# Where the first three pieces of the last modulation are made: in the retention's third head, or beside the collecting of the first layer's expert results

## The chip, the cores and the metric

The kernel runs on one core of one Trainium2 chip, in one launch. The metric is the device time of that launch in microseconds. A core has TensorE (PE in the profile), with its weight loads shown apart as PEld, VectorE (DVE), ScalarE (ACT), GpSimd (POOL) and SyncE (SP), which here only issues DMAs. Sixteen DMA engines move data between the chip's memory and the on-chip buffers.

## The reference, cut to what matters

Two blocks follow each other on 512 tokens of width 1024. The first has forgetting attention with a hierarchical mixture of experts (layer 0), then retention with a second mixture (layer 1). The second block has two layers with adaptive modulation, and a context of 256 tokens beside them.

```python
# first block, each layer i
h = h + mixer_i(rms_norm(h, norm_mix[i]))        # forgetting attention, then retention
h = h + hier_moe(rms_norm(h, norm_ffn[i]), ...)  # 32 experts, each token goes to two of them

# second block
sc, sc_ctx = jax.nn.silu(c), jax.nn.silu(c_ctx)
for layer in range(DEPTH):
    mod = sc @ ada_w[layer] + ada_b[layer]       # 1024 x 3072 weights: shift, scale, gate
    shift, scale, gate = jnp.split(mod[:, None, :], 3, axis=-1)
    mod_c = sc_ctx @ ada_w[layer] + ada_b[layer]
    ...
    u = rms_norm_2(h, norm_g[layer]) * (1 + scale) + shift
```

The modulation depends on `c_2`, `c_ctx_2` and `ada_w_2` alone. It can be made at any time before the second block reads it. `ada_w_2[1]`, the modulation of the last layer, is 12 MB in float32, and the kernel makes it in six pieces of 512 columns (2 MB each), numbered 0 to 5.

## The kernel before, in words

**Stages.** The program is a list of stages (`timeline`). `run` (L3242) goes through them on each of PE, ACT, DVE and POOL: at the start of a stage an engine waits until the other engines are done with the stage before (less a slack that some stages have), then it does its part, drains and counts itself done. SP has no such waits: it works through the `sp` parts in order, and what it issues waits by itself for the semaphores that free the destination.

**The weight ring.** Mixer weights pass through a ring of three slots of 2 MB. `Weights.add` gives a unit its number in the order of use. `Weights.load` (L232) waits until the unit three before it has been read, and then issues the DMA (L236). All loads come from SP, so they are issued in that order, behind one another. The experts' stage uses the same three slots beside five in `arena`; for the units behind it `freed` says that a slot is free once the last expert weight in it has been read. For the first of the three slots that is the down projection of expert 30, for the others the two halves of the up projection of expert 31.

**Products.** A `Products` stage holds jobs: PE fills a PSUM bank (`fill`), and DVE or ACT takes it (`take`). PE works through the jobs in their order and so does each taker.

**One piece of modulation** (`modulation`, L2578) is two jobs, both taken by DVE. `rows`: 32 matmuls of 32 columns of weights (`cmod`) against 128 of the piece (L2590; the profile has 64, two for each in float32), then a copy of the 128x128 result into `XT` (L2593), in one of two buffers. The second, whose place in the order the caller chooses: PE turns the copy (L599), and DVE adds the bias into `modc` (L2598). Filling frees the ring slot.

**Order around the change.** Layer 0 ends with `Experts` (32 experts, 64 rows each, weights streamed from memory). PE's last work there is the down projections of experts 30 and 31 (L2184); ACT copies each result (L2282), POOL scatters it to `y_dram` (L2156), and ACT's part of the stage ends when the scatters of experts 30 and 31 have landed. ACT also stores the context's gate projection (`context_z`, 1 MB) at the end. Then comes `CombineNorm` (`cb0`): SP waits for the experts' stage to be done (L2361) and fetches the results in four pieces of 1 MB, one for each tile of 128 tokens (L2364). DVE adds both expert rows to `H` (L2390, two instructions for each tile), ACT squares, DVE makes the root, both scale the rows, PE turns them (L2413) and ACT and DVE write them to `XT`. Then the retention begins.

**The retention** goes head by head: the stage `ret{h}` projects values and gate (twelve or more groups of 16 matmuls, L689), the stage `rn{h}` makes the retention itself (from L2704 on) with the next head's queries and keys in between, and `ro{h}` projects out (L818). In the third head (h = 2) pieces 0, 1 and 2 of the modulation stand among the projections. In the last head's `rn3` pieces 3, 4 and 5 stand in the retention, in the order rows, rows, turn, rows, turn, turn.

Of the kernel before, what the change touches and what calls it, by code (L numbers as in the profile page):

```python
# [23 lines left out]
KC = D // P  # L24
# [7 lines left out]
RET_H, RET_DK, RET_DV = 4, 256, 512  # L32
# [90 lines left out]
def build(nc, io):  # L123
    ctx = ExitStack()
    with ctx:
# [117 lines left out]
        class Stage:  # L243
# [25 lines left out]
            def pe(self, pe): pass  # L269
# [3 lines left out]
            def sp(self, sp): pass  # L273
# [2092 lines left out]

        class CombineNorm(Combine):


            ROWS, JUNK = region(2 * NT * D, NT, D), region(3 * NT * D, D)  # L2370

# [14 lines left out]
            def dve(self, dve):  # L2386
                for t in range(NT):
                    dve.wait_ge(self.s(f"got{t}"), self.at(f"got{t}") + 16)
                    for k in range(2):
                        i = dve.scalar_tensor_tensor(H[:, t, :], self.YG[:, t, k, :], gates[:, k, t:t + 1], H[:, t, :], ALU.mult, ALU.add)  # L2390
                        if k == 0:
                            dve_step.then(dve, i)
                    i.then_inc(self.s("summed"), 1)
                for g in range(2):
                    w = slice(2 * g, 2 * g + 2)
                    ms, t_, y, r = (st[:, j, w] for j in range(4))
                    dve.wait_ge(self.s("squares"), 2 * g + 2)
                    dve_step.then(dve, dve.tensor_scalar(ms, ms, 1.0 / D, EPS, ALU.mult, ALU.add))
                    root_of(dve, ms, y, t_, r)
                    dve.nop().then_inc(self.s("rstd"), 1)  # L2400
                    t = 2 * g + 1
                    dve.tensor_scalar(self.ROWS[:, t, :], H[:, t, :], st[:, 3, t:t + 1], None, ALU.mult).then_inc(self.s("rows_v"), 1)
                for c in range(1, KC, 2):
                    dve.wait_ge(self.s("turned"), c + 1)
                    dve.tensor_scalar(XT[:, c, 0:SEQ], bank(c), cols[:, V_MIX + KC + c:V_MIX + KC + c + 1], None, ALU.mult)

            def pe(self, pe):
                for t0 in range(0, NT, 2):
                    pe.wait_ge(self.s("rows_a"), t0 // 2 + 1)
                    pe.wait_ge(self.s("rows_v"), t0 // 2 + 1)  # L2410
                    for c in range(KC):
                        for t in range(t0, t0 + 2):
                            i = pe.transpose(bank(c)[:, t * P:(t + 1) * P], self.ROWS[:, t, c * P:(c + 1) * P], ident)  # L2413
                        if t0 + 2 == NT:
                            i.then_inc(self.s("turned"), 1)
# [128 lines left out]
        def use_units(stage, *us):  # L2544

            def sp(eng):
                for u in us:
                    Weights.load(eng, u)
            stage.sp = sp
# [123 lines left out]
        def moe(layer, after):  # L2673
            route = next(stage for stage in timeline if stage.tag == ("fo1", "ro3")[layer])
            lane = ContextValues("late", 1) if layer else ContextMixing("early", 0)
            Experts(f"ex{layer}", layer, after, route, lane.inline())
            (CombineNorms if layer else CombineNorm)(f"cb{layer}", lane)


        R_ROT, R_DEC = region(20480, 2, SEQ), region(21504, RET_H, SEQ)  # L2680
# [87 lines left out]
        def retention():  # L2768
            w = io["ret_w_in"][0]

            def modulation_unit(q):
                return Weights.add((0, KC, 512, io["ada_w_2"][1][:, 512 * q:512 * (q + 1)]))

            def qk_unit(h):
                return Weights.add((0, KC, 256, w[:, 256 * h:256 * (h + 1)]), (2048, KC, 256, w[:, D + 256 * h:D + 256 * (h + 1)]))

            def queries_keys(p, qk, tables=None, then=None, lead=False):
                sevens.split += (qk,)

                def turn_pairs(dve, s, m, sums, plus):  # L2780

                    if tables and (s, m) == (0, 0):
                        dve.wait_ge(*tables)
                    if plus is not None:
                        dve_step.then(dve, dve.tensor_tensor(R_SUM, sums, plus, ALU.add))
                        sums = R_SUM
                    cos, sin = (R_ROT[:, a, 256 * s:256 * (s + 1)].unsqueeze(1).broadcast_to([P, 2, 256]) for a in range(2))
                    dve.tensor_tensor(R_COS, sums, cos, ALU.mult)
                    dve_step.then(dve, dve.tensor_tensor(R_SIN, sums, sin, ALU.mult))
                    dst = (R_Q, R_K)[m][:, :, 256 * s:256 * (s + 1)]  # L2790
                    dve.tensor_tensor(dst[:, 0, :], R_COS[:, 0, :], R_SIN[:, 1, :], ALU.subtract)
                    return dve.tensor_tensor(dst[:, 1, :], R_SIN[:, 0, :], R_COS[:, 1, :], ALU.add)
                sevens.unit(qk, False, hook=turn_pairs, then=then, lead=lead)

            quad = lambda at: region(at, 4, 256)
            sevens = Sevens((quad(13312), quad(14336), quad(19456), quad(2048)), quad(24576), quad(25600))
            for h in range(RET_H):
                p = Products(f"ret{h}")
                last = h == RET_H - 1
                modulated = h == RET_H - 2  # L2800
                qk = [] if h else [qk_unit(0)]
                m0 = modulation_unit(0) if modulated else None
                uv = Weights.add((0, KC, 512, w[:, 2 * D + 512 * h:2 * D + 512 * (h + 1)]))
                m1 = modulation_unit(1) if modulated else None
                ug = Weights.add((0, KC, 512, w[:, 4 * D + 512 * h:4 * D + 512 * (h + 1)]))
                m2 = modulation_unit(2) if modulated else None
                use_units(p, *(u for u in (*qk, m0, uv, m1, ug, m2) if u is not None))
                if h == 0:
                    loads(p, (R_ROT, io["rot"]), (R_DEC, io["decay"]))
                    sevens.split += (qk[0],)  # L2810
                    sevens.begin(p).weight_sums(qk[0], tokens=True)
                    queries_keys(p, qk[0], (p.s("small"), p.at("small") + 32), lambda: sevens.weight_sums(uv), True)
                else:
                    sevens.begin(p).weight_sums(uv)
                if last:
                    p.pool = lambda pool: route_weights(pool, 1)
                if modulated:
                    turned = modulation(p, m0, 1, 0)
                sevens.unit(uv, True, whole(R_V), then=lambda: sevens.weight_sums(ug), lead=(h > 0))
                if modulated:  # L2820
                    turned()
                    turned = modulation(p, m1, 1, 1)
                sevens.unit(ug, True, whole(R_G), func=ACT.Silu)
                if modulated:
                    turned()
                    modulation(p, m2, 1, 2)()

                inner = Products(f"rq{h}", width=4).inline()
                if not last:
                    qk = qk_unit(h + 1)  # L2830
                    use_units(inner, qk)
                    sevens.split += (qk,)
                    sevens.begin(inner).weight_sums(qk)
                    lead = len(inner.jobs)
                    queries_keys(inner, qk)
                    first = sevens.middle
                else:
                    lead = 0
                    ms = [modulation_unit(3 + i) for i in range(3)]
                    use_units(inner, *ms)  # L2840
                    turned = None
                    for i, m in enumerate(ms):
                        then = modulation(inner, m, 1, 3 + i)
                        if turned:
                            turned()
                        turned = then
                    turned()
                    first = len(inner.jobs)
                r = Retain(f"rn{h}", h, inner, lead, first)
                u = Weights.add((0, 4, D, io["ret_w_out"][0][512 * h:512 * (h + 1), :]))  # L2850
                where = dict(bank0=4, ready=r.laid())
                o = RouteProj("ro3", 1, u, 4, R_YT, **where) if last else OutProj(f"ro{h}", u, 4, R_YT, NT, **where)
                o.slack = {("pe", "dve"): 1}
                use_units(o, u)
# [436 lines left out]
```

## Time and profile before

| | |
|---|---|
| median of 3 runs | 2964.3 us (2963.15 to 2972.04) |
| the profiled execution | 2958.9 us |
| its span | 2957.1 us |
| PE, PEld, DVE, ACT, POOL busy | 91%, 59%, 39%, 22%, 10% |
| mean granted TensorE clock | 0.966 |
| moved by DMA | 610 MB, mean 206 GB/s |

The times of all rows are microseconds from the start of the span. A releaser behind an arrow is what ended the idle time before an instruction. A share of the chain of waits says how much of the span hangs on an engine: PE has 74% of it, DMA 11% and DVE 6%.

### The profile page before, as it was taken

What the parts mean: (1) busy time and instruction counts of PE and PEld (TensorE: products, weight loads), DVE (VectorE), ACT (ScalarE), POOL (GpSimd) and SP (SyncE); (2) the same over time, 40 slices, a digit from 0 to 9 for tenths busy, and PEclk for the clock granted to TensorE, in tenths of its full rate; (3) what the DMA queues carried; (4) which work ended last, traced back from release to release, by engine and by line L of the source; (5) the groups of instructions that cost most, each with busy time, mean ns of one, the idle gap of its engine ahead of it and who ended that gap; (6) DMA issues with size and microseconds to landing.
All of it is one profiled execution on the core that took longest, in us unless ns stands there. A gap on an engine that the chain in (4) does not pass through costs nothing.

```text
span 2957.1 us, 35044 instructions
## 1 busy us (share of the span) xinstructions
PE 2686.4 (91%) x14222; PEld 1738.8 (59%) x14222; DVE 1140.6 (39%) x2541; ACT 640.4 (22%) x1316; POOL 289.8 (10%) x280
## 2 busy tenths in 40 slices
PE   7999979999999699999979989997699998999998
PEld 5858743554444476776743444443577667865864
DVE  4344441112122544424341111110755455665566
ACT  2130421123222100100020010000353341043053
POOL 2002000111110000001000111110200001212211
PEclk9999989999999899999989999999899999999999
DMA  5603248999998521232378999997310111320310
GB/s 182 263 10 136 115 183 353 417 414 414 378 417 364 212 86 63 80 126 101 133 289 363 421 420 420 416 419 329 124 45 31 66 38 57 97 82 14 112 26 36
DMA packets 115354, 610.19 MB, mean 206 GB/s; under 512 B 13148, under 2 KB 25500, under 8 KB 88432
## 3 DMA queue, kind: packets, MB, share of 16 engines
q1 hardware_dynamic: 92000, 541.98, 46.0%
q0 software_dynamic: 20512, 54.76, 5.5%
q10 hardware_dynamic: 2672, 11.09, 1.0%
q8 instruction: 117, 1.92, 0.3%
q14 instruction: 53, 0.43, 0.0%
HBM read 588.84 MB, written 35.65 MB: 211 GB/s over the span
## 4 chain that ended last, share of the span: by engine, by line
PE 74%; DMA 11%; DVE 6%; PEld 3%; issue 2%; ACT 2%; POOLq 0%; PEldq 0%; SPq 0%; DVEq 0%; ACTq 0%; POOL 0%
PE psum L689 24%; PE psum L2172 12%; PE psum L2184 6%; DMA ring<-in_expert_w_gu 6%; PE psum L818 6%; PE psum L944 5%; PE psum L589 4%; DMA arena<-in_expert_w_gu 4%; PE psum L973 3%; PE psum L962 3%; PE psum L579 2%; PE psum L1239 2%; PEld psum L689 2%; PE psum L2165 1%; PE psum L2178 1%
## 5 line engine op out<-in xcount | busy, mean ns | idle before, releaser
L2172 PE MATMUL psum<-ring,XT 128*64 128x512 f32 x1024 | 242.1, 612 | 24.1 <-DMA ring<-in_expert_w_gu 21.1
L2172 PE MATMUL psum<-arena,XT 128*64 128x512 f32 x1024 | 237.9, 608 | 15.7 <-DMA arena<-in_expert_w_gu 15.6
L2243 DVE TENSOR_TENSOR XT<-XT,psum 64x512 f32<-64x512 f32 x64 | 44.1, 690 | 529.5 <-ACT XT L2246 529.5
L689 PE MATMUL psum<-arena 128*128 128x256 f32 x1056 | 238.7, 379 | 0.0
L689 PEld LDWEIGHTS psum<-arena 128*128 128x128 f32 x1056 | 200.3, 190 | 27.1
L944 PE MATMUL psum<-arena 64*128 64x384 f32 (+7 forms) x736 | 187.4, 473 | 27.1 <-ACT arena L998 16.2
L689 PE MATMUL psum<-XT,ring 128*128 128x256 f32 x864 | 195.3, 380 | 5.3 <-DVEq L3250 5.3
L689 PEld LDWEIGHTS psum<-XT,ring 128*128 128x128 f32 x864 | 163.3, 190 | 32.2 <-issue 6.8
L2172 PEld LDWEIGHTS psum<-ring,XT 128*64 128x64 f32 x1024 | 74.8, 140 | 168.5 <-issue 129.6
L818 PE MATMUL psum<-ring,arena 128*128 128x512 f32 x384 | 166.6, 593 | 4.4 <-DVEq L3250 2.0
L2172 PEld LDWEIGHTS psum<-arena,XT 128*64 128x64 f32 x1024 | 76.7, 139 | 154.5 <-issue 131.7
L998 ACT ACTIVATE arena<-psum,rt 128x768 f32<-128x768 f32 (+4 forms) x192 | 144.0, 750 | 44.0 <-DVE rt L3157 26.1
L986 ACT ACTIVATE arena<-psum 128x512 f32<-128x512 f32 (+3 forms) x304 | 133.1, 477 | 92.7 <-PE psum L962 91.2
L2156 POOL DMA_INDIRECT y_dram<-XT,lists x64 | 64.5, 1008 | 868.1 <-ACT XT L2282 840.7
L2246 ACT ACTIVATE XT<-psum 64x512 f32<-64x512 f32 x64 | 37.8, 590 | 506.9 <-PE psum L2172 506.9
L962 PE MATMUL psum<-cst,arena 128*128 128x128 f32 x880 | 135.6, 282 | 10.8 <-DVE arena L1042 5.8
L709 ACT ACTIVATE XT<-psum 128x512 f32<-128x512 f32 x33 | 19.7, 597 | 579.4 <-PE psum L689 579.4
L689 PE MATMUL psum<-ring,XT 128*128 128x256 f32 x624 | 141.0, 380 | 3.9 <-DVEq L3250 2.9
L962 PEld LDWEIGHTS psum<-cst,arena 128*128 128x128 f32 x880 | 99.5, 143 | 57.0 <-issue 31.6
L689 PEld LDWEIGHTS psum<-ring,XT 128*128 128x128 f32 x624 | 118.0, 190 | 22.3 <-PEq L3250 3.6
L689 PE MATMUL psum<-ring,arena 128*128 128x256 f32 x576 | 129.5, 379 | 1.0 <-DVEq L3250 1.0
L689 PE MATMUL psum<-arena,ring 128*128 128x256 f32 x576 | 130.2, 379 | 0.0
(382 smaller groups left out, 3779.2 us busy)
## 6 DMA issues: line engine op xcount, KB each, us to landing
ring<-in_expert_w_gu SPq DMA_DIRECT2D x64, 2048.0 KB, 19.1
arena<-in_expert_w_gu SPq DMA_DIRECT2D x64, 2048.0 KB, 20.3
arena<-in_expert_w_down SPq DMA_DIRECT2D x32, 2048.0 KB, 13.6
ring<-in_expert_w_down SPq DMA_DIRECT2D x32, 2048.0 KB, 12.5
ring<-in_ada_w SPq DMA_DIRECT2D x12, 2048.0 KB, 8.5
ring<-in_fox_w_in SPq DMA_DIRECT2D x8, 2048.0 KB, 12.8
ring<-in_ret_w_in SPq DMA_DIRECT2D x8, 2048.0 KB, 10.5
ring<-in_c_in_w SPq DMA_DIRECT2D x8, 2048.0 KB, 7.7
```

Source lines behind the costliest of these rows:

```text
L579: i = pe.matmul(ps[0][0:cols_[1] - cols_[0], 0:ntok], w[:, c, cols_[0]:cols_[1]], x[:, c, tok:tok + ntok], start=(c == 0), stop=(c == k - 1))
L589: i = pe.matmul(ps[0][:, 0:width], x[:, c, t * P:(t + 1) * P], w[:, c, c0:c0 + width], start=(c == 0), stop=(c == k - 1))
L689: m = pe.matmul(ps[0][:, 2 * P * i:2 * P * (i + 1)], x, w, start=(not onto and i == 0 and c == 0), stop=(c == 3), skip_group_check=True)
L818: i = pe.matmul(bank(self.bank0 + n % 4), self.x[:, c, t * P:(t + 1) * P], w[:, c, half * BANK:(half + 1) * BANK], start=(c == 0), stop=(c ...
L944: ins = pe.matmul(self.s_at(n, c0, c1), lhsT, rhs, start=True, stop=True)
L962: i = pe.transpose(bank(b)[:, j * P:(j + 1) * P], self.P[:, u % 4, (k0 + j) * P:(k0 + j + 1) * P], ident)
L973: ins = pe.matmul(psum[hh * DH:(hh + 1) * DH, (6 + pair % 2) * BANK + i * P:(6 + pair % 2) * BANK + (i + 1) * P], v(h + hh, kt), self.PT[: ...
L986: act.activation(self.PT[:, m % 2, u % 2, k0:k0 + k, :], bank(b)[:, 0:k * P].rearrange("p (k q) -> p k q", k=k), ACT.Copy)\
L998: act.activation(self.P[:, n % 4, 0:hi - lo], self.s_at(n, lo, hi), ACT.Exp, bias=sm[:, 0, n:n + 1], accum_out=sm[:, 1, n:n + 1]).then_inc ...
L2156: pool.indirect_dma_start(self.y_halves, at, self.Y[e % 2], None, bounds_check=4 * SEQ - 1, oob_is_err=False)\
L2172: i = pe.matmul(psum[side * BR:(side + 1) * BR, 0:FF], x[:, 4 * part + c, :], w[:, c, side * FF:(side + 1) * FF], start=(part == 0 and c = ...
L2184: i = pe.matmul(psum[half * BR:(half + 1) * BR, 5 * BANK:6 * BANK], self.HT[:, c, :], w[:, c, half * BANK:(half + 1) * BANK], start=(c == ...
```

## The change

The class `CombineNorm` gets three new steps, and the third head of the retention loses its three pieces. The pieces keep their matmuls, copies, turns and bias adds.

- SP: the three 2 MB loads are issued before SP waits for the experts' stage, and so ahead of the four fetches of the results.
- DVE: the six steps of the three pieces stand right behind the sum of the first tile.
- PE: the fills and turns stand at the start of its part of `cb0`, and it waits until all have been taken before it turns the normed rows. Their order is that of `rn3`: rows 0, rows 1, turn 0, rows 2, turn 1, turn 2.

```diff
         class CombineNorm(Combine):
 
+            def sp(self, sp):
+                for m in self.ms:
+                    Weights.load(sp, m)
+                super().sp(sp)
...
                     i.then_inc(self.s("summed"), 1)
+                    if t == 0:
+                        self.modulations.dve(dve)
...
             def pe(self, pe):
+                self.modulations.pe(pe)
+                self.modulations.all_taken(pe)
                 for t0 in range(0, NT, 2):
...
-            (CombineNorms if layer else CombineNorm)(f"cb{layer}", lane)
+            c = (CombineNorms if layer else CombineNorm)(f"cb{layer}", lane)
+            if not layer:
+
+                c.ms = [Weights.add((0, KC, 512, io["ada_w_2"][1][:, 512 * q:512 * (q + 1)])) for q in range(3)]
+                c.modulations = Products("modulations").inline()
+                turned = None
+                for q, m in enumerate(c.ms):
+                    then = modulation(c.modulations, m, 1, q)
+                    if turned:
+                        turned()
+                    turned = then
+                turned()
...
-                modulated = h == RET_H - 2
                 qk = [] if h else [qk_unit(0)]
-                m0 = modulation_unit(0) if modulated else None
                 uv = Weights.add((0, KC, 512, w[:, 2 * D + 512 * h:2 * D + 512 * (h + 1)]))
-                m1 = modulation_unit(1) if modulated else None
                 ug = Weights.add((0, KC, 512, w[:, 4 * D + 512 * h:4 * D + 512 * (h + 1)]))
-                m2 = modulation_unit(2) if modulated else None
-                use_units(p, *(u for u in (*qk, m0, uv, m1, ug, m2) if u is not None))
+                use_units(p, *qk, uv, ug)
...
-                if modulated:
-                    turned = modulation(p, m0, 1, 0)
                 sevens.unit(uv, True, whole(R_V), then=lambda: sevens.weight_sums(ug), lead=(h > 0))
-                if modulated:
-                    turned()
-                    turned = modulation(p, m1, 1, 1)
                 sevens.unit(ug, True, whole(R_G), func=ACT.Silu)
-                if modulated:
-                    turned()
-                    modulation(p, m2, 1, 2)()
```

## Rows read from the trace of the kernel before

**Rows 1.** Chain of waits, end of experts to first retention matmul: start, length, what.
```profile
974.67 0.43 PE psum L2184
...
976.28 3.67 PE psum L2184 x16
...
979.97 0.61 ACT XT L2282
...
981.36 4.77 DMA y_dram<-XT,lists
...
986.82 4.75 DMA arena<-y_dram
...
993.02 2.49 DVE H L2390 x2
...
1000.57 1.28 DVE H L2390
...
1012.89 2.18 PE psum L689 x9
```
**Rows 2.** Timeline of that stretch: start, length, engine, line, operation, count, idle before.
```profile
980.03 0.33 ACTq L1945 DMA_DIRECT2D context_z<-arena  x1
...
986.82 2.23 SPq L2364 DMA_DIRECT2D arena<-y_dram  x4
989.10 13.13 SPq L236 DMA_DIRECT2D ring<-in_ret_w_in  x4
991.70 10.16 DVE L2390 SCALAR_TENSOR_TENSOR H<-arena,gates,H 128x1024 f32<-128x1024 f32 x8 [15.52 <-DMA arena<-y_dram]
```
**Rows 3.** Timeline, third head's projections, first and last PE instruction of the three pieces.
```profile
1273.75 1.95 PE L2590 MATMUL psum<-ring,cmod 128*32 128x128 f32 x64 [0.98 <-POOLq L3250]
...
1329.68 4.55 PE L2704 MATMUL psum<-arena 128*128 128x512 f32 x16 [0.50 <-DVEq L3250]
```
**Rows 4.** Timeline, second head's projections, which hold no modulation.
```profile
1155.42 7.15 PE L689 MATMUL psum<-ring,XT 128*128 128x256 f32 x32 [1.01 <-POOLq L3250]
...
1205.53 4.55 PE L2704 MATMUL psum<-arena 128*128 128x512 f32 x16 [1.53 <-ACTq L3250]
```
**Rows 5.** Timeline, pieces 3 to 5 in the last head, from the first fill on.
```profile
1461.08 3.70 PE L2590 MATMUL psum<-ring,cmod 128*32 128x128 f32 x128
...
1468.03 0.48 DVE L2593 COPY XT<-psum 128x128 f32<-128x128 f32 x2
...
1468.77 3.64 PE L2590 MATMUL psum<-ring,cmod 128*32 128x128 f32 x64
...
1472.48 0.29 DVE L2593 COPY XT<-psum 128x128 f32<-128x128 f32 x1 [2.60 <-PE psum L2590]
...
1473.34 0.17 DVE L2598 TENSOR_TENSOR modc<-psum,adab 128x8 f32<-128x8 f32 x1 [0.32 <-PE psum L599]
```
**Rows 6.** Stretches: length, busy of PE PEld DVE ACT POOL, clock, DMA share, GB/s.
```profile
10.00:15.00 5.00, 0.00 (x0) 0.00 (x0) 3.60 (x11) 2.08 (x4) 0.00 (x0) 1.00 1.05 387
...
975.00:980.00 5.00, 4.37 (x21) 1.82 (x20) 0.42 (x1) 0.62 (x2) 0.99 (x1) 1.00 0.09 27
980.00:987.00 7.00, 0.00 (x0) 0.00 (x0) 0.00 (x0) 0.57 (x1) 0.98 (x1) 0.68 0.45 176
987.00:992.00 5.00, 0.00 (x0) 0.00 (x0) 0.30 (x1) 0.00 (x0) 0.00 (x0) 0.50 0.84 300
...
480.00:600.00 120.00, 118.53 (x582) 58.69 (x580) 18.23 (x37) 17.38 (x33) 15.68 (x16) 1.00 1.00 412
...
1465.00:1470.00 5.00, 1.64 (x25) 1.33 (x29) 4.43 (x9) 0.00 (x0) 3.87 (x4) 0.72 1.01 414
```
**Rows 7.** Stretch in which the retention's first weights land, same columns.
```profile
1012.80:1020.00 7.20, 7.11 (x33) 6.32 (x34) 7.05 (x7) 0.60 (x1) 1.16 (x2) 1.00 0.91 345
```
**Rows 8.** Scatters of results (L2156) while experts' weights stream: time to landing.
```profile
DMA to landing us min/median/max: 7.0/8.1/13.4
```
**Rows 9.** The retention's four first weight DMAs (L236, from 989.10 on): time to landing.
```profile
DMA to landing us min/median/max: 13.0/15.9/17.0
```

## Prediction

> **What bounds the kernel now.** I read the chain of waits first, because PE is busy for 91% of the span while the change moves PE work. The question is in which of the two places PE sets the pace. In the chain around the collecting of the experts' results PE drops out. It ends its last down projection at 979.95. From there the chain runs through ACT's copy, the last scatter to `y_dram` (4.77 us), the fetch of the first tile's results (4.75), the eight sums on DVE, the root and the scaling. PE comes back for its turns, and the retention's first matmul is at 1012.89 [rows 1]. So DMA and DVE bound this stretch, and PE's time in it is free. The timeline shows how tight DVE is there: eight sums are busy for 10.16 us, one after another from 991.70 on, and none waits for a later tile [rows 2]. The stretches show what the DMA engines do: 27 GB/s at 975 to 980, 176 until 987, 300 until 992 [rows 6].
>
> In the third head it is the other way round. The chain there is matmul after matmul, and each piece stands between two groups of projections. Whatever PE doesn't do there shortens the program.
>
> **What is removed.** I compare the third head's projections with the second's, which are the same without the pieces. From the first PE instruction to the first matmul of the retention proper the third takes 1329.68 - 1273.75 = 55.93 us [rows 3], the second 1205.53 - 1155.42 = 50.11 [rows 4]. The difference, **5.82 us**, holds the three fills, the turns and the last wait for DVE. It also holds what comes back: without the pieces the next matmul waits 1.5 us for ACT's last gate instead of 0.5. DVE's copies and adds lie beside matmuls there and give nothing of their own. SP loses three loads from a place where PE waits for no weight, so nothing there either. Removed: -5.8.
>
> **What is added to the DMA queue.** The three loads wait only until their ring slots have been read. The latest needed for the first is the down projection of expert 30, whose end is the ready signal at about 975.1 [rows 1]. So 6144 KB are issued from about 975.2 on, while the four fetches can't be issued before all is done at 986.8 [rows 2]. They are issued by the same engine, so I take it that the first fetch moves only after the weights. What must pass the sixteen DMA engines by the time the first tile has landed is then 6144 KB of weights, 1024 KB of `context_z` (issued at 980.03, rows 2), two scatters of 256 KB and 1024 KB of the tile: 8704 KB, or 8.91 MB. The first tile alone shows the fixed part: 4.75 us for 1.05 MB, which at 387 GB/s is 2.7 of moving and 2.0 of latency.
>
> The rate is the unknown. A stretch at the start in which SP loads the same kind of units, 2 MB in rows of 2 KB, ran at 387 GB/s; with experts' weights and scatters mixed it was 412 over 120 us [rows 6]. I take 387, since the weights that dominate here are of that kind. 8.91 / 0.387 = 23.0 us, so the first tile lands at 975.2 + 2.0 + 23.0 = 1000.2 instead of 991.6: **+8.6 us**. With 412 it is 21.6 us and +7.2. The lower bound is that only the weights stand ahead, at 420 or so (414 is the highest row, rows 6): 6.29 / 0.414 = 15.2, plus 2.0 and 2.6 for the tile, lands at 995.0, +3.4. The upper bound is the slowest stretch with weights landing, 345 GB/s [rows 7]: 25.8 us, 1003.0, +11.4.
>
> On the slack that the old order had: the DMA engines were far from full between 975 and 987 [rows 6], room for some 12 x 0.387 = 4.6 MB less the 1.4 MB that used it. The new loads are 6.3 MB. That is why the stretch can't swallow them.
>
> The last scatter (issued at 981.36) now runs beside streaming weights. Under such a stream scatters took 8.1 us in the median and 13.4 at most [rows 8] against 4.77. Then the stage is done at about 990 instead of 986.7, or 995.4 at worst. The fetch would then land at 990 + 4.75 or 995.4 + 4.75 = 1000.1, neither later than the 1000.2 that the queue gives. So this costs nothing beside the queue.
>
> At "DMA: Bandwidth & Descriptors", section "Where 436 GB/s comes from", the Trainium skill says that for transfers between memory and the on-chip buffers the memory's share, about 358 GB/s, binds. The rows of this core do not agree (387, 412, 414, rows 6). By 358 the 8.91 MB would take 24.9 us and the delay would be +10.5, the whole sum +10.2, which is slower by more than 0.3%. That is one form of rival 1 below, and I give it 0.05 of that rival's chance.
>
> **What is added to DVE.** All six DVE steps stand between the first tile's sum and the second's, and the sums are on the chain. The last head has the very same six jobs in the same order. There DVE copies rows 0 and 1 at 1468.03, PE turns, PE fills piece 2 (3.64 us), DVE copies it, PE turns, and DVE's last add ends at 1473.51 [rows 5]. That is **5.5 us** during which no other DVE work can pass. The fill of piece 2 is inside it, because in PE's order it stands behind turn 0, and that waits for DVE's first copy. The 3.64 us are at a granted clock of about half (two fills of 64 in 3.70 at the full one, rows 5). Between 980 and 987, idle, the clock fell to a mean of 0.68 and then stood at 0.50, the lower of its two levels, 1.2 GHz [rows 6]. In the new kernel PE fills pieces 0 and 1 at about 990 to 997. Then it waits for DVE, which has summed the first tile at 1000.2 + 2.6 = 1002.8. Five or six idle microseconds; the old trace fell within some 3 us of the end of work. So I take the slow fill. At 2.4 GHz the fill takes 1.9 instead of 3.6 and the steps 3.7 (the lower bound). The upper bound is 6.0: one more half-clock turn of 0.5, should PE be slow to answer the first copy. The later tiles land 2.6 us apart, so nothing of the 5.5 hides behind them.
>
> **What is late next.** The retention's first weights stand behind the fetches in the queue. They were issued from 989.10 on and took up to 17.0 us each [rows 9], and the first matmul is at 1012.89 [rows 1]. They move back by the queue's 8.6 and their first use moves back by 14, so they stay hidden. The third unit's load now waits for the fill of piece 2, near 1007, and is used some 40 us later. The turns of the normed rows are as cold as before. ACT waits for `context_z` only at the end of the stage. These edits cost nothing.
>
> **Sum.** +8.6 + 5.5 - 5.8 = **+8.3 us**. Against the profiled execution of 2958.9 that is 2967.2. The runs' median is 2964.3, 5.4 above that execution, and the change is put on it: **2972.6 us**, +0.28%. About 0.3%, here 8.9 us, is what a measurement of this kernel can tell from no change.
>
> **The rivals.**
> 1. *The stream is slower than I take it* (slower). Reads mixed with 1.5 MB of writes run like the slow stretch, 345 GB/s [rows 7]: +11.4 + 5.5 - 5.8 = +11.1 us, 2975.4. It decides from a delay of 9.2 us on, that is below 8.91 / 23.6 = 378 GB/s. For it: my forecast is only 0.6 us from the bound. Against it: the rows at full share show 387 to 414.
> 2. *PE stays at its higher clock or the queue is lighter.* The steps take 3.7 and the delay is 7.2: +5.1 us, 2969.4.
> 3. *The queue gives the fetch its turn early*, so that only part of the weights stands ahead: +3.4 + 3.7 - 5.8 = +1.3, and with the delay at nothing and the steps at 5.5, -0.3 us, 2964.0. Against it: one issuing engine, and the retention's loads of rows 9 took 13 us and more behind the fetches.
> 4. *It is faster.* That needs both added costs to vanish, as when DVE's steps fell into a wait for the second tile: -5.8 us, 2958.5, and still within 0.3%. More than that has no row behind it.
>
> **How the numbers follow.** Forecast 0.42 (+7 to +8.9), rival 1 0.34, rival 2 0.12, rival 3 0.08, rival 4 0.04. Slower by over 0.3% is rival 1, 0.34. Faster by over 0.3% gets 0.03 out of rival 4. The rest, 0.63, is within 0.3%. The range is 2964.0 to 2977.0: from rival 3 to rival 1's price with the steps' upper bound (11.4 + 6.0 - 5.8 = 11.6, 2975.9), and a little of the runs' spread.
>
> **What would show it.** The first load of `ada_w` on SP at about 975.2, and the fetches' landing at 1000 instead of 991.6. A gap in DVE's sums after the second, 5.5 us long, with the fill of piece 2 at 3.6 us in it. The first retention matmul at about 1027. Third head's projections at 50.1 us. If the fetches land before 996, the queue step is wrong; if the gap is under 4 us, the clock step is.

## The result, and the profile after

The changed kernel takes 2974.93 us in the median of 20 runs, the kernel before 2965.85 in the median of 20: a ratio of 1.0029 with a 95% interval of 1.0022 to 1.0035. That is some 8.6 us slower (6.5 to 10.4); the two medians differ by 9.1. It is about 0.3%, and on which side of 0.3% the interval leaves open. The prediction's ratio was 1.0028 (+8.3 on 2964.3). The profiled execution took 2970.7 us with a span of 2968.9; PE is busy for 2693.3 us, DVE for 1143.7, and the chain of waits over the whole span is the old one but for a per cent more of DVE (7%).

The chain of waits from the end of the experts to the first retention matmul (start, length, what), to be held against [rows 1]:

```profile
978.24 3.67 PE psum L2184 x16
...
981.93 0.60 ACT XT L2282
...
983.30 8.66 DMA y_dram<-XT,lists
...
992.66 10.54 DMA arena<-y_dram
...
1003.34 1.29 DVE H L2394
...
1006.20 0.47 PE psum L599
...
1006.67 3.57 PE psum L2598 x64
...
1011.03 0.17 DVE modc L2606
...
1012.42 2.49 DVE H L2394 x2
...
1029.98 2.18 PE psum L689 x9
```

Two links have grown. The last scatter takes 8.66 us instead of 4.77, the fetch of the first tile 10.54 instead of 4.75. And PE, which had no part in the sums, now stands between them with the fill of piece 2. This execution was already 2.0 us later when it got here, before anything that the change touches. So I count from ACT's copy of the last expert's result (979.97 before, 981.93 now). From there to the first sum it is 21.41 us against 11.73, and to the first retention matmul 48.05 against 32.92: +9.68 and +15.13.

The timeline of the same stretch (start, length, engine, line, operation, count, idle time before), against [rows 2, 5]:

```profile
977.08 5.33 SPq L236 DMA_DIRECT2D ring<-in_ada_w  x3
...
992.76 5.66 PE L2598 MATMUL psum<-ring,cmod 128*32 128x128 f32 x128 [10.87 <-ACTq L3257]
996.46 17.10 SPq L236 DMA_DIRECT2D ring<-in_ret_w_in  x4
1003.34 2.60 DVE L2394 SCALAR_TENSOR_TENSOR H<-arena,gates,H 128x1024 f32<-128x1024 f32 x2 [25.20 <-DMA arena<-y_dram]
1005.86 0.48 DVE L2601 COPY XT<-psum 128x128 f32<-128x128 f32 x2
...
1006.20 0.47 PE L599 MATMUL psum<-cst,XT 128*128 128x128 f32 x1 [7.78 <-DVE XT L2601]
...
1006.60 3.64 PE L2598 MATMUL psum<-ring,cmod 128*32 128x128 f32 x64
...
1011.11 7.63 DVE L2394 SCALAR_TENSOR_TENSOR H<-arena,gates,H 128x1024 f32<-128x1024 f32 x6
```

DVE's sums are broken between 1005.86 and 1011.11, 5.25 us, and 3.64 of them are one fill. It is [rows 5] over again. The three loads are issued from 977.08 on, as soon as the down projection of expert 30 has ended.

The third head's projections, first and last PE instruction, against [rows 3]:

```profile
1290.81 7.14 PE L689 MATMUL psum<-ring,XT 128*128 128x256 f32 x32 [0.98 <-POOLq L3257]
...
1340.92 4.33 PE L2723 MATMUL psum<-arena 128*128 128x512 f32 x14 [1.53 <-ACTq L3257]
```

50.11 us instead of 55.93: 5.82 saved, to the hundredth what the second head had shown. Stretches of the collecting (length, busy of PE, PEld, DVE, ACT, POOL, granted clock, DMA share, GB/s), against [rows 6]:

```profile
980.00:987.00 7.00, 1.89 (x10) 0.49 (x6) 0.00 (x0) 0.60 (x1) 0.98 (x1) 0.97 1.04 362
987.00:992.00 5.00, 0.00 (x0) 0.00 (x0) 0.00 (x0) 0.00 (x0) 0.00 (x0) 0.50 1.02 408
992.00:997.00 5.00, 4.24 (x84) 4.27 (x88) 0.00 (x0) 0.00 (x0) 0.00 (x0) 0.52 1.05 396
...
1003.00:1006.00 3.00, 0.00 (x0) 0.00 (x0) 2.62 (x3) 0.00 (x0) 0.00 (x0) 0.61 1.00 415
1006.00:1010.20 4.20, 4.00 (x66) 3.18 (x66) 0.51 (x3) 1.15 (x2) 0.00 (x0) 0.50 1.01 395
```

The DMA engines, at 176 and 300 GB/s in the first two stretches before, are now full all the way. The clock of PE is at its lower level (0.50, 1.2 GHz) when the fill of piece 2 runs.

### The profile page after: what moved, and what is told of

Read it like the earlier page. It is cut to its first block, busy times and chain, and to the rows that moved or that the text cites. A ratio compares the mean times of both kernels' runs of the same rounds, so it can differ in the third digit from the quotient of the medians.

```text
span 2968.9 us, 35039 instructions
## 1 busy us (share of the span) xinstructions
PE 2693.3 (91%) x14222; PEld 1746.5 (59%) x14222; DVE 1143.7 (39%) x2541; ACT 639.8 (22%) x1316; POOL 288.7 (10%) x280
## 4 chain that ended last, share of the span: by engine, by line
PE 74%; DMA 11%; DVE 7%; PEld 3%; issue 2%; ACT 2%; PEldq 0%; SPq 0%; DVEq 0%; POOLq 0%; ACTq 0%; POOL 0%
PE psum L689 24%; PE psum L2172 11%; PE psum L2184 6%; DMA ring<-in_expert_w_gu 6%; PE psum L818 6%; PE psum L944 5%; PE psum L589 4%; DMA arena<-in_expert_w_gu 4%; PE psum L973 3%; PE psum L962 3%; PE psum L579 2%; PE psum L1239 2%; PEld psum L689 2%; PE psum L2165 1%; DVE arena L1042 1%
## 5 line engine op out<-in xcount | busy, mean ns | idle before, releaser
L2172 PE MATMUL psum<-ring,XT 128*64 128x512 f32 x1024 | 242.3, 613 | 24.1 <-DMA ring<-in_expert_w_gu 21.1
L2156 POOL DMA_INDIRECT y_dram<-XT,lists x64 | 64.4, 1006 | 869.2 <-ACT XT L2282 841.8
```

The source lines that it names most:

```text
L2156: pool.indirect_dma_start(self.y_halves, at, self.Y[e % 2], None, bounds_check=4 * SEQ - 1, oob_is_err=False)\
L2172: i = pe.matmul(psum[side * BR:(side + 1) * BR, 0:FF], x[:, 4 * part + c, :], w[:, c, side * FF:(side + 1) * FF], start=(part == 0 and c = ...
```

## The experiments

All ratios are against the kernel before, timed beside it on the same chip. In the table, "first sum" and "first matmul" are the profiled times from ACT's copy of the last expert's result to DVE's first sum and to the first retention matmul. "Head" is the third head's projections, "sum" the changes of "first matmul" and "head" together, and "measured" the ratio turned into microseconds. A sum comes from one execution and is good to about a microsecond: PE's turns of the normed rows, which no edit touches, took from 5.00 us (one piece early) to 6.46 (two, steps behind). The granted clock rose at different points within them.

| kernel | first sum | first matmul | head | sum | ratio [95%] | measured |
|---|---|---|---|---|---|---|
| before | 11.73 | 32.92 | 55.93 | | | |
| changed | 21.41 | 48.05 | 50.11 | +9.3 | 1.0029 [1.0022, 1.0035] | +8.6 |
| loads alone | 21.06 | 42.10 | same | +9.2 | 1.0031 [1.002, 1.0042] | +9.2 |
| steps alone | 12.18 | 36.79 | same | +3.9 | 1.001 [1.0001, 1.002] | +3.0 |
| removal alone | 11.83 | 32.41 | 50.11 | -6.3 | 0.998 [0.997, 0.999] | -5.9 |
| steps first | 21.32 | 42.43 | 50.11 | +3.7 | 1.0007 [0.9998, 1.0015] | +2.1 |
| fills together | 21.18 | 43.41 | 50.11 | +4.7 | 1.0018 [1.0009, 1.0027] | +5.3 |
| fetch on ACT | 18.72 | 51.71 | 50.11 | +13.0 | 1.0054 [1.0041, 1.0066] | +16.0 |
| loads alone, fetch on ACT | 18.80 | 42.02 | same | +9.1 | 1.0037 [1.0023, 1.0051] | +11.0 |
| one piece early | 13.34 | 33.73 | 53.91 | -1.2 | 0.9999 [0.9989, 1.0009] | -0.3 |
| two pieces early | 18.09 | 39.39 | 51.71 | +2.3 | 1.0016 [1.0007, 1.0025] | +4.7 |
| two, steps behind | 16.05 | 38.45 | 51.71 | +1.3 | 1.0006 [0.9994, 1.0017] | +1.8 |

**Each term by itself.** The kernels loads alone, steps alone and removal alone take the sum apart.

Loads alone, put into the kernel before:

```diff
+            def sp(self, sp):
+                for m in self.ms:
+                    Weights.load(sp, m)
+                super().sp(sp)
...
+                c.ms = [Weights.add((0, KC, 512, io["ada_w_2"][1][:, 512 * q:512 * (q + 1)])) for q in range(3)]
+                for m in c.ms:
+                    Weights.freed[m] = (w_ready[m % RING], Weights.value[m])
```

> The kernel before, with three more 2 MB loads of the same pieces issued ahead of the wait for the experts' stage and read by nobody; the third head still makes the pieces. It prices the DMA queue by itself. Theory (the queue is the larger of two added costs): the first tile of the results lands 10.5 us after its issue instead of 4.75, the issue itself is some 4 us later because the last scatter takes 8.7 us instead of 4.8, and the program is +9.7 us (ratio 1.0033). Rival (the fetch would overtake part of the weights once PE and DVE leave them alone, and DVE's gap is the main cost): +3 to +5 us, ratio 1.0010 to 1.0017.

The first tile landed 10.5 us after its issue, and the ratio was 1.0031. DVE's sums stay in one piece:

```profile
994.45 1.76 SPq L2364 DMA_DIRECT2D arena<-y_dram  x4
...
1005.05 10.15 DVE L2395 SCALAR_TENSOR_TENSOR H<-arena,gates,H 128x1024 f32<-128x1024 f32 x8 [24.86 <-DMA arena<-y_dram]
```

So three loads that nobody reads cost about as much as the whole change comes to. The rival, by which DVE's gap would be the main cost, falls.

Steps alone, with units that hold no DMA:

```diff
+                c.ms = [Weights.add() for q in range(3)]
+                c.modulations = Products("modulations").inline()
...
+                    if t == 0:
+                        self.modulations.dve(dve)
...
+                self.modulations.pe(pe)
+                self.modulations.all_taken(pe)
```

> The kernel before, with the six jobs added to the collecting stage at the places that the change gives them, but with no loads: they work on what the last experts left in the three slots, and the third head then makes the pieces properly and writes over them. It prices the steps by themselves. Theory: a gap of 5.3 us between the second and third sum, as in the changed kernel, and +5.4 us in all (1.0018). But the first tile lands at 991.6 here, so PE has less idle time between its second fill (ended near 992.5) and the first turn (near 994.3). If the granted clock is still at its higher level then, the gap is near 3.7 us and the whole +3.7 (1.0013). The rival that the steps cost nothing beside DMA expects 1.0000.

The second case came: the gap is 3.4 us, from 1001.41 to 1004.82 in its timeline, and the ratio is 1.001.

```profile
993.95 4.90 PE L2599 MATMUL psum<-ring,cmod 128*32 128x128 f32 x128 [7.29 <-POOLq L3269]
...
1001.41 0.48 DVE L2602 COPY XT<-psum 128x128 f32<-128x128 f32 x2
...
1001.75 0.33 PE L599 MATMUL psum<-cst,XT 128*128 128x128 f32 x1 [2.89 <-DVE XT L2602]
1002.00 1.96 PE L2599 MATMUL psum<-ring,cmod 128*32 128x128 f32 x64
...
1004.82 7.63 DVE L2395 SCALAR_TENSOR_TENSOR H<-arena,gates,H 128x1024 f32<-128x1024 f32 x6
```

PE was idle for 2.89 us before its first turn, not 7.78 as in the changed kernel, and the same fill took 1.96 us instead of 3.64. A stretch from 1001.80 to 1004 has a granted clock of 1.00. So 1.7 us of the changed kernel's gap are a consequence of the queue: the late tile keeps PE idle until its clock has fallen. That is most of why the parts alone add up to less than the whole in the traces, +9.2 + 3.9 - 6.3 = +6.8 against +9.3. The ratios say the same, +6.3 against +8.6, but their intervals are wider than that difference.

Removal alone: the changed kernel without anything in the collecting stage. Pieces 0 to 2 are not computed, and zeros stand in their place.

```diff
+                dve.memset(modc[:, 1, 0:12, :], 0.0)
...
-                    Weights.load(sp, m)
...
-                        self.modulations.dve(dve)
...
-                self.modulations.pe(pe)
```

> The changed kernel without the loads and the steps in the collecting stage: pieces 0 to 2 of the last modulation are not computed at all, the columns hold zeros. It prices the removal from the third head by itself. Theory: the third head's projections take 50.1 us instead of 55.9, and the program is -5.8 us against the kernel before (0.9980). Rival (part of the gain comes back at the next wait, as for ACT's gate or a weight load): -2 to -4 us (0.9987 to 0.9993).

0.998, or -5.9 us (-3.0 to -8.9), as much as the 5.82 of the trace. There is no sign that any of it comes back later, but the interval still holds the rival's -3 to -4; the projections' 50.11 us in the trace speak against it.

**The gap on DVE.** Steps first:

```diff
             def dve(self, dve):
+                self.modulations.dve(dve)
                 for t in range(NT):
...
-                    if t == 0:
-                        self.modulations.dve(dve)
```

> The changed kernel with DVE's six steps ahead of its wait for the first tile instead of behind the first tile's sum. Theory: the fills of pieces 0 and 1 are done by 998, piece 2 has landed by then, and so all six steps fit into the wait that ends at 1003. The gap of 5.3 us in the sums goes, the queue's cost stays: +3.9 us against the kernel before (1.0013), 5 less than the changed kernel. Rival (piece 2 lands only just before the first tile, so its fill and the last steps stick out): 2 to 4 us of the gap stay, ratio 1.0020 to 1.0027.

The tile landed 10.1 us after its issue, at 1001.9, and the first sum starts at 1002.24: the six steps hold DVE up by 0.3 us and leave no gap behind. The ratio is 1.0007. The fill of piece 2 had to wait for its load until 999.42, so the rival was near, but the fill ran at the higher clock (1.96 us) and was done in time:

```profile
991.78 1.76 SPq L2364 DMA_DIRECT2D arena<-y_dram  x4
991.88 5.80 PE L2597 MATMUL psum<-ring,cmod 128*32 128x128 f32 x128 [10.99 <-ACTq L3256]
...
999.42 1.96 PE L2597 MATMUL psum<-ring,cmod 128*32 128x128 f32 x64 [1.48 <-DMA ring<-in_ada_w]
...
1002.24 10.14 DVE L2395 SCALAR_TENSOR_TENSOR H<-arena,gates,H 128x1024 f32<-128x1024 f32 x8
```

Fills together, with a third buffer for the copy:

```diff
-            x = M_ROWS[:, q % 2, :]
+            x = XT[:, 1, SEQ:SEQ + P] if layer == 1 and q == 2 else M_ROWS[:, q % 2, :]
...
+                for turned in [modulation(c.modulations, m, 1, q) for q, m in enumerate(c.ms)]:
+                    turned()
```

> The changed kernel with a third buffer for the copies, so that PE makes the three fills ahead of the three turns; DVE's steps stay behind the first tile's sum. Theory (the gap of 5.3 us in the sums is mostly the fill of piece 2 at half clock, which waits for DVE's first copy): the fill is done before the first tile lands, three copies and the turns are left, and the gap is 1.9 to 2.4 us. The program is 3 us shorter than the changed kernel (1.0019). Rival (semaphore round trips make most of the gap): gap of 4 us or more, ratio 1.0025.

The gap is 1.36 us (copies from 1008.82, the next sum at 1010.18), less than the 1.9 I expected at least, and the ratio 1.0018.

```profile
1008.82 0.68 DVE L2601 COPY XT<-psum 128x128 f32<-128x128 f32 x3
1009.16 0.90 PE L599 MATMUL psum<-cst,XT 128*128 128x128 f32 x3 [3.48 <-DVE XT L2601]
1009.67 0.59 DVE L2606 TENSOR_TENSOR modc<-psum,adab 128x8 f32<-128x8 f32 x3 [0.17 <-PE psum L599]
1010.18 7.63 DVE L2394 SCALAR_TENSOR_TENSOR H<-arena,gates,H 128x1024 f32<-128x1024 f32 x6
```

So the order of the jobs, a fill behind a turn that waits for DVE, made 3.9 of the 5.25 us, and the six steps themselves 1.4.

**The queue.** Fetch on ACT, otherwise the changed kernel:

```diff
             def act(self, act):
+                rows = y_dram[0:2 * SEQ, :].rearrange("(p t k) d -> p t k d", t=NT, k=2)
+                for t in range(NT):
+                    act.dma_start(self.YG[:, t, :, :], rows[:, t, :, :]).then_inc(self.s(f"got{t}"), 16)
...
-                super().sp(sp)
```

> The changed kernel with the four fetches of the results issued by ACT at the start of its part of the stage, so that they are in another queue than the weights. Theory of one queue in order (the fetch stands behind the rest of the weights): the first tile, issued near 992, lands after some 8 us instead of 10.5, and piece 2 lands later instead; the program is 1 to 3 us shorter than the changed kernel (1.0019 to 1.0026). Rival (only the bytes count, since all queues share the sixteen engines): landing within 1 us of the changed kernel's and ratio 1.0029.

The first tile landed after 7.6 us instead of 10.5, as the theory of a queue in order has it. But I was wrong on the program: 1.0054, slower by far. I had written that piece 2 would land later and not asked who waits for it. It is PE's fill, and behind that DVE in the middle of its sums:

```profile
994.95 1.77 ACTq L2378 DMA_DIRECT2D arena<-y_dram  x4
...
1002.67 2.60 DVE L2396 SCALAR_TENSOR_TENSOR H<-arena,gates,H 128x1024 f32<-128x1024 f32 x2 [22.51 <-DMA arena<-y_dram]
...
1012.48 3.62 PE L2600 MATMUL psum<-ring,cmod 128*32 128x128 f32 x64 [6.58 <-DMA ring<-in_ada_w]
...
1016.97 7.63 DVE L2396 SCALAR_TENSOR_TENSOR H<-arena,gates,H 128x1024 f32<-128x1024 f32 x6
```

Loads alone with the fetch on ACT leaves that wait out. The edit is the one above, made to the kernel with the loads alone. With it SP no longer waits for the stage's end, so the retention's first weights are issued sooner too, from 4.8 us after ACT's copy on instead of 12.3.

> The kernel before with the three unused loads ahead, and with the fetches issued by ACT in another queue. No step of a piece waits for a load here. With one queue in order the program was +9.2 us (1.0031). Theory (the engines share their time between the queues by what is waiting, so the first tile comes sooner and the later ones slower, and the same bytes end at the same time): first tile 7.6 us after its issue instead of 10.6, but DVE then waits for later tiles; first retention matmul no more than 3 us sooner, ratio 1.0022 to 1.0031. Rival (being behind the weights in one queue is the whole cost of the loads): ratio 1.0016 or less.

```profile
1008.68 2.61 DVE L2397 SCALAR_TENSOR_TENSOR H<-arena,gates,H 128x1024 f32<-128x1024 f32 x2 [22.60 <-DMA arena<-y_dram]
...
1011.81 2.60 DVE L2397 SCALAR_TENSOR_TENSOR H<-arena,gates,H 128x1024 f32<-128x1024 f32 x2 [0.52 <-DMA arena<-y_dram]
...
1015.04 2.60 DVE L2397 SCALAR_TENSOR_TENSOR H<-arena,gates,H 128x1024 f32<-128x1024 f32 x2 [0.63 <-DMA arena<-y_dram]
```

The first sum starts 2.3 us sooner than behind one queue (18.80 against 21.06), and then DVE waits for each later tile by half a microsecond. The first matmul comes 0.1 us sooner, 42.02 against 42.10. The ratio of 1.0037 lies above the range I gave, its interval covers it. So another queue didn't help: what the first tile gains, the later ones lose. How much of that is due to the retention's weights, which share here, these runs do not tell. The Trainium skill says at "DMA: Bandwidth & Descriptors", section "Issuing engines are not separate DMA queues", that DMAs run on the same sixteen engines and interleave whoever issued them, so that issuing from several saves only the time to issue. The two traces agree as to the first matmul, 42.02 against 42.10. Which transfer lands first did change with the queue: the first sum came after 18.80 us, not 21.06.

**How many pieces fit.** One piece early, with its two steps first and pieces 1 and 2 in the third head:

```diff
-                c.ms = [Weights.add(...) for q in range(3)]
+                c.ms = [Weights.add(...) for q in range(1)]
...
-                use_units(p, *qk, uv, ug)
+                use_units(p, *(u for u in (*qk, uv, m1, ug, m2) if u is not None))
```

> Only piece 0 is made beside the collecting, with DVE's two steps ahead of its wait for the first tile; pieces 1 and 2 stay in the third head. Theory (what decides is how many bytes stand ahead of the first tile against what the engines have room for): 2.1 + 1.05 + 0.52 + 1.05 = 4.7 MB take 12.8 us at 370 GB/s, done at 989.9, earlier than any fetch can land, so only the slower last scatter costs, +1.2 us; the third head gives 2.1 back. Sum -0.9 us (0.9997). Rival (every load ahead costs in proportion, a third of 9.6): +3.2 - 2.1 = +1.1 us (1.0004).

First sum +1.6 (13.34 against 11.73), third head -2.0. The whole +1.6 lies in the fetch's issue, 8.45 us after ACT's copy instead of 6.85, behind a last scatter of 6.37 us instead of 4.77; the fetch itself took 4.9. So one load costs half of what a third of the price for three would be: it fits into the room that the engines have, and only the scatter feels it. (At the first matmul +0.8 is left, because the turns took 5.00 us here and not 5.81.) The ratio, 0.9999, can't be told from no change, nor from the rival's 1.0004; only the trace speaks for the theory.

Two pieces early, with the steps first:

```diff
-                c.ms = [Weights.add(...) for q in range(3)]
+                c.ms = [Weights.add(...) for q in range(2)]
...
-                use_units(p, *qk, uv, ug)
+                use_units(p, *(u for u in (*qk, uv, ug, m2) if u is not None))
```

> Pieces 0 and 1 are made beside the collecting, DVE's four steps ahead of its wait for the first tile; piece 2 stays in the third head. Theory of the bytes: 4.2 + 1.05 + 0.52 + 1.05 = 6.8 MB take 18.4 us at 370 GB/s, the first tile lands near 995.5, +4.0 us; the third head gives 4.1 back. Sum 0 (1.0000). Rival in proportion: +6.4 - 4.1 = +2.3 us (1.0008).

1.0016, nearer to the rival, but not for its reason. The fetches were issued at 994.64 and the first took 4.8 us, so the tile was there at 999.5. DVE came to it at 1001.95:

```profile
994.64 1.99 SPq L2364 DMA_DIRECT2D arena<-y_dram  x4
994.74 6.35 PE L2597 MATMUL psum<-ring,cmod 128*32 128x128 f32 x128 [10.92 <-ACTq L3260]
...
1001.86 0.17 DVE L2605 TENSOR_TENSOR modc<-psum,adab 128x8 f32<-128x8 f32 x1 [0.22 <-PE psum L599]
1001.95 10.14 DVE L2395 SCALAR_TENSOR_TENSOR H<-arena,gates,H 128x1024 f32<-128x1024 f32 x8
```

The fills, mostly at the lower clock, last until 1001.1, and now the steps hold up the sums. Two, steps behind, puts the four steps back behind the first tile's sum:

```diff
-                self.modulations.dve(dve)
                 for t in range(NT):
...
+                    if t == 0:
+                        self.modulations.dve(dve)
```

> Pieces 0 and 1 beside the collecting as before, but DVE's four steps back behind the first tile's sum. In the form with the steps first, the tile landed 4.9 us after its issue and DVE was still held by the steps, 2.4 us longer, because PE's two fills ran at half clock until then. Theory: the tile's landing sets the start (+4.0), the steps make a gap of 1.2 us, the third head gives 4.2: +1.0 us (1.0003), 2 to 4 us less than the form with the steps first. Rival (the two loads themselves cost the 6.4 us): no change against that form, 1.0016.

The first sum starts after 16.05 us (+4.3), the gap is 1.0 us, the ratio 1.0006. So the loads of two pieces cost 4.3, where the sum of bytes said 4.0, and the rest was the order. But 4.0 of them lie in the fetch's later issue, 10.89 us after ACT's copy instead of 6.85, behind a scatter of 8.82 us; the fetch itself took 5.0.

No version beats the kernel before by more than its measurement tells. The collecting has room for the load of about one piece, at 1.6 us on the first sum.

## Why the prediction was right, point by point

- *Removal, -5.8.* 5.82 in the trace, -5.9 measured by itself. Right.
- *Queue, +8.6.* The first sum came 9.7 us later, by loads alone 9.3. The term is 1.1 too small. It was counted as 8.91 MB at 387 GB/s. The loads were issued from 977.08 on and the tile landed at 1003.2: less 2.0 of latency 24.1 us, which would be 370 GB/s. The stretches of that time, however, run at 396 to 421, all but the first, which has 362. What was mis-sized is the bytes, as the queues from 977.08 to 1003.20 show (q1 carries what SP issues, q0 the scatters):

```profile
DMA packets 3667, 9.49 MB, mean 363 GB/s; under 512 B 174, under 2 KB 174, under 8 KB 3312
...
q1 hardware_dynamic: 3357, 8.10, 83.7%
...
q0 software_dynamic: 160, 0.27, 2.7%
```

Over 24.1 us the 9.49 MB make 394 GB/s, near the rate that was taken. SP's queue had moved 8.10 MB and not the 7.34 of three loads and one tile, so 0.8 MB of what stands behind the first tile had moved before it had landed. (The scatters went the other way, 0.27 MB and not the 0.52 counted.) The likeliest reason is that the sixteen engines don't finish one transfer before they begin the next, and a tile has landed only with its last part. That reason is argued, not shown. The memory's share of about 358 GB/s that the Trainium skill gives ("DMA: Bandwidth & Descriptors", section "Where 436 GB/s comes from") isn't the reason: this stream ran at up to 421.
- *Rival 1.* Its own bound was a delay of 9.2 us, or 378 GB/s, and the trace has 9.7 and 370. By that sign it came; by its mechanism, a slower stream, it didn't.
- *The scatter, nothing beside the queue.* It took 8.66 us, expected were 8.1, and the fetch was issued 10.7 us after ACT's copy instead of 6.85. That is 3.9 of the 9.7, but by this trace an earlier issue would have won little: the third load, issued at 978.1, took 22.2 us and landed at about 1000.3, only 2.9 before the tile. So the queue was last, as said.

```profile
L236 SPq DMA_DIRECT2D ring<-in_ada_w x3: 397/566/4268, 977.1 to 978.1; - x3
...
DMA to landing us min/median/max: 9.6/17.4/22.2
```

With two pieces the tile landed 4.8 us after its issue, as in the kernel before, so there the late scatter and stage end carry the cost. The second load landed some 2.6 us before the tile in that trace, so the two bounds fall together, and that the bytes alone gave the right 4.0 is partly luck.
- *DVE's steps, +5.5.* 5.25 in the trace. The row of the last head was the right one, and its clock too (PE idled 7.8 us before, where five or six were forecast). Steps alone shows the lower bound, 3.7, as a case of its own: 3.4 us with PE idle for less than 3. The one small thing left out: the turns of the normed rows began 0.2 us further from the first matmul (7.70 against 7.50).
- *What was costed at nothing.* The retention's weights, ACT's wait for `context_z` and the cover of the third unit cost nothing: from the sums' end to the first matmul nothing but those 0.2 is added.
- *Sum.* +9.7 + 5.25 + 0.2 - 5.8 = +9.3 in the profiled execution; its span grew by 11.8, of which 2.0 came ahead of the change. The 20 runs give +8.6. The forecast was +8.3, with +7 to +8.9 for its case. The runs lie in that, the trace beyond it. So the mechanism was right in each term, and that the number came so close is partly luck: the queue was 1.1 too small, the steps 0.25 too large, and the runs give 0.7 less than the trace. The interval reaches over 0.3%, so on which side of it the kernel is stays open.
- *The chances.* Rival 4 was priced at -5.8 us, within 0.3%, with no row for more, and yet 0.03 of its 0.04 went to faster than that. The measured slowdown rules both out.

## What to carry to other kernels

Where an engine idles because all wait for a small transfer, the stretch isn't free for work that must be loaded: count the bytes that the DMA engines still have room for (here some 3 MB, one load of three), and put no more ahead of the transfer. Count also a part of what stands behind it, here 0.8 MB. When steps are inserted into an engine's chain, look at what else the partner engine does between two of them; a fill behind a turn made three quarters of the gap here, and one more buffer or another place took it away. Before a transfer is moved back in favour of another, name who waits for the one that is moved.

## What the runs showed of the hardware

A transfer issued on ACT beside a full queue of SP landed 7.6 us after its issue, where one behind that queue took 10.5, at about the same total rate (394 to 417 GB/s against 396 to 421). The third weight load paid for it: it landed 32.3 us after its issue, not 22.2 as with one queue.

The clock of PE fell after different idle times. In the kernel before it fell within some 3 us of the last matmul, and in fills together too: the mean is 0.84 over the 3.4 us between fill and turns, and the turns ran at 0.50. In the changed kernel it was still at 1.00 over 4.5 us without a matmul:

```profile
998.50:1003.00 4.50, 0.00 (x0) 0.00 (x0) 0.00 (x0) 0.00 (x0) 0.00 (x0) 1.00 1.04 421
```

and then 0.61 on average from 1003 to 1006. A fill of 64 matmuls took 1.96 us at 1.00 and 3.64 at 0.50. So in these traces 3 to 5 idle microseconds ended either way, and the length of the idle time alone doesn't tell the clock behind it.
